# One ring of 22 places for the expert weights, each refilled when it comes free

## The reference

```
def hier_moe(xn, w_group, b_group, w_sub, b_sub, w1, w3, w2):
...
    combine = jnp.einsum('tk,tke->te', g_w * top_p, jax.nn.one_hot(expert_id, N_EXPERTS, dtype=jnp.float32))
    out = jnp.zeros((b * s, d), jnp.float32)
    for e in range(N_EXPERTS):
        hid = jax.nn.silu(t @ w1[e]) * (t @ w3[e])
        out = out + combine[:, e:e + 1] * (hid @ w2[e]).astype(jnp.float32)
```

## Time and profile before

| | |
|---|---|
| median of 3 runs | 1160.44 us (1155.7 to 1162.52) |
| profiled execution | 1156.09 us |
| its span, first to last instruction | 1154.3 us |
| granted clock of TensorE, mean | 0.978 |
| TensorE matmuls busy | 1060.9 us (92%) |
| VectorE, ScalarE busy | 401.7 us, 333.2 us |
| moved by DMA | 238.14 MB, mean 206 GB/s |

### The profile page before, as it was taken

How to read it: one execution, slowest core, us unless ns; L and a number is a source line. 1 busy time by engine, 2 the same in 40 slices (tenths; PEclk the granted TensorE clock), 3 DMA queues, 4 the chain that set the end, 5 groups by cost and what they waited for, 6 DMA issues and landing times.

```text
span 1154.3 us, 13587 instructions
## 1 busy us (share of the span) xinstructions
PE 1060.9 (92%) x4960; PEld 673.4 (58%) x4960; DVE 401.7 (35%) x1180; ACT 333.2 (29%) x779; POOL 13.7 (1%) x60
## 2 busy tenths in 40 slices
PE   3899999999989999999999988889999898998886
PEld 0344554444367768678888456678888643443332
DVE  2349264342249544523831024641112400000004
ACT  2222143341143454234553034630011311111102
POOL 0000000000000000000000000000000000000010
PEclk9899999999989999999999999999999899999998
DMA  9896218442143313443444432056444589999995
GB/s 370 330 372 246 73 36 326 164 171 73 69 146 110 110 37 116 181 146 110 150 162 156 152 110 74 1 220 252 148 146 146 231 367 420 422 424 423 423 423 214
DMA packets 32906, 238.14 MB, mean 206 GB/s; under 512 B 3697, under 2 KB 3953, under 8 KB 6769
## 3 DMA queue, kind: packets, MB, share of 16 engines
q1 hardware_dynamic: 28768, 204.48, 45.5%
q10 hardware_dynamic: 3504, 30.80, 7.1%
q0 software_dynamic: 576, 2.10, 0.5%
HBM read 232.65 MB, written 19.40 MB: 218 GB/s over the span
## 4 chain that ended last, share of the span: by engine, by line
PE 78%; DMA 12%; ACT 4%; DVE 3%; issue 1%; SPq 1%; ACTq 0%; DVEq 0%
PE lin L434 30%; DMA ring<-w_stream 10%; PE aux L434 9%; PE lin L516 8%; PE sc L457 6%; PE lin L813 6%; PE aux L718 3%; PE aux L813 3%; DMA PT<-w_stream 3%; PE sc L552 2%; PE lin L565 2%; PE sc L772 2%; PE aux L578 2%; PE sc L487 1%; ACT S L1000 1%
## 5 line engine op out<-in xcount | busy, mean ns | idle before, releaser
L434 PE MATMUL lin<-H,ring 128*128 128x256 f32 (+1 forms) x1360 | 343.6, 414 | 5.3 <-ACT H L1041 3.8
L434 PEld LDWEIGHTS lin<-H,ring 128*128 128x128 f32 x1360 | 262.2, 194 | 84.8 <-issue 50.5
L813 PE MATMUL lin<-ring,PR 128*64 128x512 f32 x400 | 92.8, 613 | 17.4 <-DMA ring<-w_stream 16.4
L516 PE MATMUL lin<-ring,H 128*128 128x512 f32 (+2 forms) x256 | 90.1, 513 | 0.0
L434 PE MATMUL aux<-Y,ring 128*128 128x512 f32 (+1 forms) x256 | 85.2, 494 | 4.2 <-DVE Y L1417 3.1
L813 PEld LDWEIGHTS lin<-ring,PR 128*64 128x64 f32 x400 | 31.7, 140 | 76.6 <-issue 76.6
L434 PEld LDWEIGHTS aux<-Y,ring 128*128 128x128 f32 x256 | 48.9, 192 | 39.5 <-issue 32.0
L516 PEld LDWEIGHTS lin<-ring,H 128*128 128x128 f32 x256 | 46.3, 190 | 42.7 <-issue 30.1
L457 PE MATMUL sc<-H,ring 128*128 128x512 f32 (+1 forms) x192 | 70.8, 503 | 0.0
L990 ACT ACTIVATE PT<-lin 128x512 f32<-128x512 f32 (+3 forms) x96 | 43.8, 467 | 92.8 <-PE lin L565 92.7
L1365 DVE SCALAR_TENSOR_TENSOR UN<-UN,cols 128x512 f32<-128x512 f32 (+1 forms) x120 | 64.5, 611 | 0.0
(11 more groups left out here) (237 smaller groups left out, 1028.8 us busy)
## 6 DMA issues: line engine op xcount, KB each, us to landing
ring<-w_stream SPq DMA_DIRECT2D x153, 1024.0 KB, 6.9
Y<-w_stream SPq DMA_DIRECT2D x14, 1024.0 KB, 15.6
UN<-w_stream SPq DMA_DIRECT2D x12, 1024.0 KB, 18.6
S<-w_stream SPq DMA_DIRECT2D x6, 1024.0 KB, 19.3
PT<-w_stream SPq DMA_DIRECT2D x6, 1024.0 KB, 20.9
rows<-PR ACTq DMA_DIRECT2D x7, 512.0 KB, 7.9
cb<-c_in ACTq DMA_DIRECT2D x2, 1152.0 KB, 8.1
X<-x_in SPq DMA_DIRECT2D x2, 1024.0 KB, 8.5
```

The source lines that it names most:

```text
L434: m = mm(dst, w[:, k, :], rhs(k), start=n == 0, stop=n == KT - 1)
L516: m = mm(bank[:, 0:width], src[:, k, tt * P:(tt + 1) * P], w[k // 4][:, k % 4, 0:width], start=k == 0, stop=k == KT - 1)
L813: m = mm(bank[c, :], left[:, 4 * half + k, c], w[x][:, k, :], start=half + k == 0, stop=last)
```

## The change

All expert units go through one ring of `PLACES` = 22 places in reading order: unit n of the 96 lies in place n modulo 22. Places 13 to 18 are the six of the old ring; the sixteen others are dead buffers: MORE (a new name over WF), UN (two), SP (three, S and PT laid side by side), two parts of PR, CW (two, over cb, wfour and SC), X1, Y (two), H1, NB (RS, RI, SA and RT side by side) and X0. A few small tensors are moved to make room (CX has its own, SW and SWT go to X1, `YG` to Y). ScalarE issues eleven loads instead of seven, SyncE the others. The unit n is loaded when unit n - 22 has been read. TensorE has pairs 0 to 5 unrolled, pair 6 in a loop of `turns` rounds (one here), and the last pair by itself; SyncE's refills are unrolled up to unit 93 (`AGAIN` = 94).

```diff
-RINGED = (SLOTS, SLOTS + 2, SLOTS)
+PLACES, RING_AT = 22, 13
+AGAIN = PAIR_UNITS * (PAIRS - 2) + PLACES
...
+        ASIDE = {
+            0: MORE[:, 0:2048], 1: UN[:, 0:2048], 2: UN[:, 2048:4096], 3: SP[:, 0:2048], 4: SP[:, 2048:4096], 5: SP[:, 4096:6144],
+            6: E1[:, 6144:8192], 7: E1[:, 8192:10240], 8: CW[:, 0:2048], 9: CW[:, 2048:4096], 10: X1[:, 0:2048],
+            11: Y1[:, 0:2048], 12: Y1[:, 2048:4096], 19: H1[:, 0:2048], 20: NB[:, 0:2048], 21: X0[:, 0:2048]}
+        aside_in = {n: sem(f"aside_in{n}") for n in ASIDE}
...
+        def place_of(n):
+
+            place = n % PLACES
+            if place in ASIDE:
+                return ASIDE[place], aside_in[place], n // PLACES + 1
+            slot = (BASE + place - RING_AT) % SLOTS
+            return ring[:, slot, :, :].rearrange("p b n -> p (b n)"), unit_in[slot], len(range(slot, BASE, SLOTS)) + n // PLACES + 1
...
                 def unit(j):
...
+                    n = PAIR_UNITS * (i if isinstance(i, int) else PAIRS - 1 if last else PAIRS - 2) + j
+                    w, landed, rounds = place_of(n)
+                    if not last:
+                        pe.wait_ge(landed, 16 * (rounds + late))
+                    elif n < AGAIN:
+                        pe.wait_ge(landed, 16 * rounds)
+                    else:
+                        pe.wait_ge(landed, 16 * (rounds - 1) + 16 * late)
+                    return w.rearrange("p (k n) -> p k n", n=512)
...
-            experts(0)
-            experts(1)
+            for i in range(PAIRS - 2):
+                experts(i)
             pe.wait_ge(pairs_in, 1)
+            turns = pe.value_load(NP[0:1, 2:3], min_val=1, max_val=PAIRS * (PASSES - 1) + 1)
             last_pair = pe.value_load(NP[0:1, 1:2], min_val=PAIRS - 1, max_val=PAIRS * PASSES - 1)
-            with pe.Fori(2, last_pair) as i:
-                experts(i)
-            experts(last_pair, last=True)
+            with pe.Fori(0, turns) as late:
+                experts(late + (PAIRS - 2), late)
+            experts(last_pair, turns, last=True)
...
             sp.wait_ge(aux_ready, turn["branch", KT - 1, 2] + 1)
-            for n in (2, 3):
-                load_expert(0, SLOTS + n, n)
+            for n in (RING_AT - 2, RING_AT - 1):
+                load_expert(BASE + n, n)
             for u in range(head // SLOTS * SLOTS, head):
                 sp.wait_ge(unit_free, u - SLOTS + 1)
                 load(u, u % SLOTS)
+            for n in range(RING_AT, RING_AT + SLOTS):
+                sp.wait_ge(unit_free, BASE + n - RING_AT - SLOTS + 1)
+                load_expert(BASE + n, n)
             sp.wait_ge(aux_ready, turn["out2", KT - 1] + 1)
...
+            load_expert(BASE + PLACES - 3, PLACES - 3)
+            sp.wait_ge(lin_ready, turn["ffn"] + 1)
+            load_expert(BASE + PLACES - 2, PLACES - 2)
+            sp.wait_ge(lin_ready, turn["residual"])
+            load_expert(BASE + PLACES - 1, PLACES - 1)
+            for n in range(PLACES, AGAIN):
+                sp.wait_ge(unit_free, BASE + n - PLACES + 1)
+                load_expert(BASE + n, n)
 
             sp.wait_ge(pairs_in, 1)
...
+            for n in range(AGAIN, PAIRS * PAIR_UNITS):
+                sp.wait_ge(unit_free, BASE + PAIR_UNITS * (last_pair - 1) + n - AGAIN + 1)
+                load_expert(BASE + n, n)
...
-            for n in (0, 1, 4, 5, 6, 7, 8):
-                u = BASE + SLOTS + n if n < SLOTS else BASE + PAIR_UNITS + RINGED[1] + n - SLOTS
-                act.dma_start(ASIDE[n], w_stream[u].rearrange("p b n -> p (b n)")).then_inc(aside_in[n // 2], 16)
+            for n in range(RING_AT - 2):
+                act.dma_start(ASIDE[n], w_stream[BASE + n].rearrange("p b n -> p (b n)")).then_inc(aside_in[n], 16)
...
+            dve.wait_ge(merged, KT)
             step(v.memset(PX[:, :, :], -1.0))
...
             step(v.tensor_scalar(NP[:, 0:1], CN[:, 4:5], float(PAIRS), None, ALU.add))
+            step(v.tensor_scalar(NP[:, 2:3], CN[:, 4:5], 1.0, None, ALU.add))
```

More of the change, by code:

```diff
@@ L180, in build @@
         Y = sb("Y", [P, 16, SEQ])
-        RS = sb("RS", [P, 512])
-        RI = sb("RI", [P, 512])
+        NB = sb("NB", [P, 2048])
+        RS, RI, SA = (NB[:, n:n + 512] for n in (0, 512, 1024))
+        RT = NB[:, 1536:2048].rearrange("p (b n) -> p b n", b=2)
         MOD = sb("MOD", [P, DEPTH, ADA, 2])
@@ L189, in build @@
         ST = sb("ST", [P, 4, 4])
-        S = sb("S", [P, 4, 772])
-        PT = sb("PT", [P, 4, 768])
+        SP = sb("SP", [P, 4 * 772 + 4 * 768])
+        S = SP[:, 0:4 * 772].rearrange("p (b n) -> p b n", b=4)
+        PT = SP[:, 4 * 772:].rearrange("p (b n) -> p b n", b=4)
         SQ = sb("SQ", [P, 2, 512])
-        SA = sb("SA", [P, 512])
-        RT = sb("RT", [P, 2, SEQ])
         c0 = sb("c0", [P, N_C0])
-        cb = sb("cb", [P, N_C1])
-        wfour = sb("wfour", [P, DEPTH, 2, 256])
-        WF = sb("WF", [P, DEPTH, 2, 2, 256])
+        CW = sb("CW", [P, 4096])
+        cb = CW[:, 0:N_C1]
+        wfour = CW[:, N_C1:N_C1 + 1024].rearrange("p (l f n) -> p l f n", l=DEPTH, f=2)
+        SC = CW[:, N_C1 + 1024:N_C1 + 1280].rearrange("p (k n) -> p k n", k=KT)
+        MORE = sb("MORE", [P, 2048])
+        WF = MORE.rearrange("p (l c f n) -> p l c f n", l=DEPTH, c=2, f=2)
+        CX = sb("CX", [P, TT * EC]).rearrange("p (t n) -> p t n", t=TT)
         wsmall = sb("wsmall", [P, KT, 24])
-        NP = ctx.enter_context(nc.sbuf_tensor("NP", [P, 2], mybir.dt.int32))
+        NP = ctx.enter_context(nc.sbuf_tensor("NP", [P, 3], mybir.dt.int32))
         IW = sb("IW", [P, TT, 8])
@@ L237, in build @@
         SEL = E1[:, 5632:5888].rearrange("p (t n) -> p t n", t=TT)
[L238 to L243, removed]
+        PX = E1[:, 5888:5888 + TT * EC].rearrange("p (t n) -> p t n", t=TT)
+        MK1 = E1[:, 6032:6064].rearrange("p (t n) -> p t n", t=TT)
+        CN = E1[:, 6064:6072]
+        SW = X1[:, 0:256].rearrange("p (t n) -> p t n", t=TT)
+        SWT = X1[:, 256:512]
         XT = H[:, 0, :, :].rearrange("p k n -> p (k n)").rearrange("p (t n) -> p t n", t=TT)
-        YG = [a[:, n:n + D] for a in (X1, H[:, 1, :, :].rearrange("p k n -> p (k n)")) for n in (0, D)]
+        YG = [Y.rearrange("p t n -> p (t n)")[:, q * D:(q + 1) * D] for q in range(4)]
         GAIN = SQ.rearrange("p b n -> p (b n)")
@@ L259, in build @@
         sc = ctx.enter_context(nc.psum_tensor("sc", [P, 2, 1024], F32))
[L262 to L266, removed]
+        Y1, X0, H1 = (x.rearrange("p k n -> p (k n)") for x in (Y, X[:, 0, :, :], H[:, 1, :, :]))
+        ASIDE = {
[3 more added lines that the diff above has]
+        aside_in = {n: sem(f"aside_in{n}") for n in ASIDE}
         unit_in = [sem(f"unit_in{i}") for i in range(SLOTS)]
         unit_free = sem("unit_free")
+        def place_of(n):
[4 more added lines that the diff above has]
+            return ring[:, slot, :, :].rearrange("p b n -> p (b n)"), unit_in[slot], len(range(slot, BASE, SLOTS)) + n // PLACES + 1
         cols_in_s, c0_in_s, consts_in, mem_in_s, c2_in_s, out_s = (
@@ L781, in _, with experts @@
             assert at["owed"] == 0
-            def experts(i, last=False):
-                ringed = RINGED[i] if isinstance(i, int) else RINGED[2]
+            def experts(i, late=0, last=False):
                 def unit(j):
[L788 to L803, removed]
+                    n = PAIR_UNITS * (i if isinstance(i, int) else PAIRS - 1 if last else PAIRS - 2) + j
[7 more added lines that the diff above has]
+                    return w.rearrange("p (k n) -> p k n", n=512)
                 def both(bank, left, n_k, j0, done):
@@ L875, in _, with load_expert @@
                     load(SLOTS * r + slot, slot)
[L877 to L888, removed]
+            def load_expert(u, n):
+                w, landed, _ = place_of(n)
+                src = w_stream[u] if isinstance(u, int) else w_stream[bass.ds(u, 1)].rearrange("u p b n -> (u p) b n")
+                sp.dma_start(w.rearrange("p (b n) -> p b n", b=UNIT), src).then_inc(landed, 16)
             sp.wait_ge(aux_ready, turn["branch", KT - 1, 2] + 1)
-            for n in (2, 3):
-                load_expert(0, SLOTS + n, n)
+            for n in (RING_AT - 2, RING_AT - 1):
+                load_expert(BASE + n, n)
             for u in range(head // SLOTS * SLOTS, head):
@@ L904, in _ @@
[L904 to L917, removed]
@@ new lines, in _ @@
+            sp.wait_ge(lin_ready, turn["residual"])
[3 more added lines that the diff above has]
+                load_expert(BASE + n, n)
+            sp.wait_ge(pairs_in, 1)
+            last_pair = sp.value_load(NP[0:1, 1:2], min_val=PAIRS - 1, max_val=PAIRS * PASSES - 1)
+            with sp.If(last_pair > PAIRS - 1):
+                with sp.Fori(PAIRS - 1, last_pair) as i:
+                    for j in range(PAIR_UNITS):
+                        sp.wait_ge(unit_free, BASE + PAIR_UNITS * (i - 1) + j + 1)
```

(1 more changed line is left out.)

16 lines of the change are left out of this document (1 added, 15 removed).

## The result

The kernel with 22 places takes 1144.44 us, median of four runs (1138.76 to 1145.86), against 1158.07 us (1154.38 to 1162.52) for the kernel before on the same chip: a ratio of 0.9872, 95% interval 0.9839 to 0.9904. A second set of runs on another occasion gave 0.9849 (0.9822 to 0.9876). Forecast: 1143. The profiled execution takes 1144.23 us with a span of 1142.3, 12.0 less than the span before.

The account below looks back on a forecast made before the run. The prediction took the expert stage's weight stream as the bound: -14.9 - 3.9 + 2.0 + 1.7 = -15.1 us, so 1141.0 us profiled and 1143 as median, its own range 1137 to 1148, overall 1134 to 1153.

Parts of the forecast that it names:

- What bounds the kernel: Expert stage: its end is set by the bytes to move after 920 us and holes in that stream; TensorE needs 30 us less.
- Six units, 14.9 us: Expert stream: 22 units instead of 16 in place or under way at the first pair, 74 left of 80, 14.9 us less.
- The hole, 3.9 us: Expert stream at 940 to 950 us: the hole from SyncE's order of waits goes with the new refill order, 3.9 us back.
- the missing 5.5 us: Expert stream, 217.5 us against 212.0 at full rate: the difference was put down to the start (1.4) and the hole (3.9).
- ScalarE's issues, +2.0: Before the gates' sigmoids at 763 us: four more loads on ScalarE's queue add 2.0 us, all on the path (bounds 1.8 and 2.6).
- The clock behind it, +1.7: Behind TensorE's gap near 767 us, grown to 3.7 us: a spell at 1.2 GHz costs 1.7 us (bounds 0 and 3.4).
- The bigger burst and SyncE's order at no cost: From 763 us: eleven MB at once beside the ring's loads, and SyncE's loads waiting for the last branch product, cost 0.
- TensorE never waits in pairs 0 to 6, and unrolled code costs nothing: Expert stage: no waits for weights before the last pair; unrolled code 0, at worst 1 us a pair; late-code-or-slower-stream rival 0.12.
- The gathers are hidden: Last pair: row gathers into Y, shares added by 1125.3, 3 us of cover; rival that gathers end last 0.09.
- The 14.8 us behind it stay: After the last unit lands: matmuls, combination, norm and store take 14.8 us as before.
- The last load issued near 1075 and landing some 50 us later: Sign in the profile after: the last load is issued near 1075 and lands near 1124 us.
- The number: Whole kernel: -15.1 us, profiled execution 1156.09 to 1141.0; the median put between two scales at 1143.

Follow-up runs that it names:

- places16: The changed kernel with 16 places instead of 22, in the new refill order, ScalarE issuing eight loads; 1158.79 us, ratio 0.9999 to the kernel before.
- gapwarm: The changed kernel with eight matmuls into an unread bank filling TensorE's gap before the second branch product; ratio 0.9884 to the kernel before.
- late11: The changed kernel with ScalarE's eleven loads issued behind the first six sigmoids of the gates instead of ahead; 1138.53 us, ratio 0.9829 to the kernel before.
- again22: The changed kernel measured once more without any edit; 1142.69 us, ratio 0.9849 to the kernel before.

## Why the prediction was right, step by step

*What bounds the kernel.* Right. The end moves with the bytes left after the first pair has begun: 223.6, 218.7, 211.7 and 204.05 us for 80 units in the old order, and 80, 77 and 74 in the new.

*Six units, 14.9 us.* Measured 14.66 from places16 to the changed kernel; the full windows of the kernel after show 421 to 429 GB/s. The 358 GB/s of the Trainium skill ("DMA: Bandwidth & Descriptors", section "Where 436 GB/s comes from") would have given 17.6: page and trace differ, and the trace decides.

*The hole, 3.9 us.* Measured 223.59 - 218.71 = 4.9 with the number of places unchanged, of which the window of the hole explains 3.7. The two together are 19.5 instead of 18.8. In the working two figures are slightly off, without effect on the sum: by 938 us the stream had finished 18/2.479, that is 7 units and not 8, and the missing 5.5 us are named only up to 5.3.

*ScalarE's issues, +2.0.* TensorE's gap grows by 2.14 us. Right. The lower bound of 1.8 left out the shortest of the seven issues: four of 0.33 us would be 1.3. *The clock behind it, +1.7.* This term was mis-sized: 2.6 us here (9.73 less 7.14 for the 32 matmuls), within the bounds of 0 and 3.4. The granted clock there is 0.50 (772 to 777 us), and gapwarm rules out the transfers. *The bigger burst and SyncE's order at no cost:* the stretch without ScalarE's issues is 131.50 us with eleven loads and with seven, to the hundredth. Right.

*TensorE never waits in pairs 0 to 6, and unrolled code costs nothing.* Right, by the table of waits. The DMA table has more on the queue "instruction" in this stage, 9 packets (0.15 MB) where the kernel before has 4 (0.07 MB), but the first pair takes 25.17 us as before, and each pair behind it 24.95. *The gathers are hidden.* Right: VectorE adds the last share from 1126.01 to 1127.30 us (forecast 1125.3), and then waits 4.24 us for TensorE's last product. Of this cover 1.7 us are the slow matmuls of the tail.

```profile
1126.01 1.29 DVE L1633 SCALAR_TENSOR_TENSOR H<-Y,ROWS,H 128x1024 f32<-128x1024 f32 x1 [1.18 <-DMA Y<-rows,IDX]
1131.54 0.69 DVE L1637 COPY PR<-aux 128x512 f32<-128x512 f32 x1 [4.24 <-PE aux L817]
```

*What the prediction missed.* "The 14.8 us behind it stay": counted from the last 16 matmuls they are 14.6 before, and became 16.3 in six of the nine profiled executions of the new stream that have no fill there, and in none of the three of the old. The last 16 matmuls can run partly at 1.2 GHz (5.35 us instead of 3.65, granted clock 0.72 from 1126 to 1132 us), and by then they are the path. The length of the wait ahead of them does not decide it: in the kernel after it is 1.94 us, in late11 it is 3.81, and there they run at full pace. What decides stays open. The last two groups of 16 in late11:

```profile
1117.80 3.65 PE L817 MATMUL aux<-SP,PR 128*64 128x512 f32 x16 [2.03 <-DMA SP<-w_stream]
1125.26 3.65 PE L817 MATMUL aux<-PR 128*64 128x512 f32 x16 [3.81 <-DMA PR<-w_stream]
```

*"The last load issued near 1075 and landing some 50 us later"* was wrong too, without effect: it is issued at 1093.02. Its place is free at 1075.6, and SyncE issues late for another reason, below.

*The number.* The sum was -15.1 us for the profiled execution, and 12.0 were measured there. The 3.1 us between them are +2.1 ahead of the branches, +1.65 in the tail and -0.9 in the routing, none of which the prediction has, +1.0 of issues and clock (4.7 for 3.7), and -0.7 of the stream (19.5 for 18.8). The median of 1144.44 lies so near to the forecast of 1143 in part by luck: that number was put between two scales, and not added up. The two pairs of medians have 13.6 and 17.2 us. The profiles' 12.0 is smaller than both; the old kernel's profiled run is among its quicker ones (1156.09, of 1153.4 to 1164.2), and the new one's is at its median.

## What to carry to other kernels

When a stage is bound by a full stream, count the bytes that are still to be moved when it begins: each dead buffer that can take a unit earlier is worth one unit's time, here 2.3 to 2.55 us for a unit of 1.05 MB (from 16 to 19 and from 19 to 22 places). That must end where the consumer becomes the bound, which no run here reached. Refill in the order of the frees, on a queue that works in order. Then look at what the additional issues stand in front of: four more loads ahead of a sigmoid cost 4.7 of the 19.5 us, and moving all eleven behind six sigmoids took 6.8 us off that stretch, of which 4.2 showed in the medians.

## What the runs showed of the hardware

**Issues on SyncE's queue take longer once some ten of its loads are under way.** From about 1001 us on, an issue takes mostly 2.1 us and up to 6.3, even when its place is free (start, us, loads):

```profile
1067.61 2.10 SPq L886 DMA_DIRECT2D H<-w_stream  x1
1069.76 2.10 SPq L886 DMA_DIRECT2D NB<-w_stream  x1
1071.91 2.28 SPq L886 DMA_DIRECT2D X<-w_stream  x1
...
1091.90 3.17 SPq L886 DMA_DIRECT2D PR<-w_stream  x2
```

In the earlier trace rows two issues on this queue take 0.80 us together. Counted by the landings in the trace of the kernel after, from 915 us on: the 38 issues that began with at most nine earlier loads still on their way took 0.33 to 0.73 us each, and the 37 that began with ten to twelve took 0.33 to 6.26 us, 2.1 in the median. The last load lands 32.9 us after its issue; less the gathers (2.10 MB, 5.0 us) and a row store (1.2 us) that is 26.7 us of stream, or 10.8 units. So SyncE appears to be held when ten to eleven of these loads are under way. It does no harm here, as the stream is full. That the number of loads is the cause was only read from the traces; no run changed it by itself.

**A store on another queue is not held up by this.** The row stores on ScalarE's queue land in 7.8 us (median) while the units need 22 to 28 (medians by buffer). The Trainium skill, "DMA: Bandwidth & Descriptors", section "Queues, rings and completion order", has each DMA engine take turns between the queues; the trace agrees.

```profile
MORE<-w_stream SPq DMA_DIRECT2D x4, 1024.0 KB, 21.9
rows<-PR ACTq DMA_DIRECT2D x7, 512.0 KB, 7.8
H<-w_stream SPq DMA_DIRECT2D x3, 1024.0 KB, 27.4
NB<-w_stream SPq DMA_DIRECT2D x3, 1024.0 KB, 27.8
```

**The clock's spells are a large part of the difference between executions.** In the same code the branches and the expert stage repeat within 0.3 us. The routing differs by 2 us and the tail by 1.7, both by where TensorE runs at 1.2 GHz. The part ahead of the branches differs by up to 7 us. There the mean granted clock lies between 0.93 and 0.96 from 260 to 350 us and between 0.93 and 1.00 from 700 to 750 us, by the execution, in both kernels; 90 x 0.03 and 50 x 0.07 are 2.7 and 3.5 us, an estimate. Over the 21 executions of the kernel before that were measured beside again22, the time falls as the mean granted clock rises (correlation -0.73).
